# Two of a quad's four weight sums made by an accumulating DMA instead of VectorE, in the MLP of a hybrid decoder block

## The reference, cut to what matters

```python
D_MODEL, SEQ, D_FF = 2048, 256, 4 * 2048
...
u = rmsnorm(h, norm_ff_pre[l])
f = jnp.square(jax.nn.relu(u @ w_ff1[l])) @ w_ff2[l]   # (256, 8192) @ (8192, 2048), float32
h = h + rmsnorm(f, norm_ff_post[l])
```

## Time and profile before

| | us |
|---|---|
| median of three runs | 1325.41 |
| the three runs | 1325.34 to 1327.75 |
| the profiled execution, its own time | 1325.52 |
| its span, first to last instruction | 1323.7 |
| TensorE busy | 1311.4 |
| VectorE busy | 928.1 |
| ScalarE busy | 671.0 |

### The profile page before, as it was taken

One profiled execution on the slowest core, in us unless ns is written; L12 is line 12 of the kernel. 1 busy time (PEld: TensorE's weight loads), 2 busy tenths in 40 slices (PEclk: granted clock), 3 DMA queues, 4 the chain that ended last, 5 costly groups with the idle time before them and its releaser, 6 DMA issues.

```text
span 1323.7 us, 18258 instructions
## 1 busy us (share of the span) xinstructions
PE 1311.4 (99%) x6998; PEld 1116.4 (84%) x6998; DVE 928.1 (70%) x1265; ACT 671.0 (51%) x922; POOL 47.0 (4%) x92
## 2 busy tenths in 40 slices
PE   9999999999999999999999999999999999999998
PEld 8889999888888888889987888877888877888886
DVE  7766565687875555557768976579876699776554
ACT  7554453456664443454645664445454455545442
POOL 1222110000000000000000000000000000000000
PEclk9999999999999999999999999999999999999999
DMA  9766555555566666674755666646576465766653
GB/s 315 205 185 170 170 163 149 167 167 155 170 194 188 185 188 221 226 246 148 219 159 188 214 219 191 195 156 207 190 223 189 146 207 191 229 188 190 223 195 104
DMA packets 135209, 252.56 MB, mean 191 GB/s; under 512 B 8275, under 2 KB 45551, under 8 KB 134748
## 3 DMA queue, kind: packets, MB, share of 16 engines
q1 hardware_dynamic: 131216, 241.40, 58.6%
q0 software_dynamic: 2160, 4.74, 1.8%
q10 hardware_dynamic: 1756, 5.36, 1.1%
HBM read 249.29 MB, written 2.17 MB: 190 GB/s over the span
## 4 chain that ended last, share of the span: by engine, by line
PE 90%; DVE 6%; ACT 2%; DMA 1%; issue 0%; ACTq 0%; SPq 0%; DVEq 0%
PE bank L2006 16%; PE bank L1696 11%; PE bank L1698 11%; PE bank L1697 11%; PE bank L2009 8%; PE bank L1742 4%; PE bank L2056 4%; PE bank L2057 4%; PE bank L2058 4%; PE bank L1730 3%; PE bank L1731 3%; PE bank L1729 3%; PE bank L1744 2%; DVE b_lo L1536 2%; DVE s_lo L1541 1%; ACT b_hi L873 1%
## 5 line engine op out<-in xcount | busy, mean ns | idle before, releaser
L1017 DVE TENSOR_TENSOR w_lo<-raw,w_hi 128x1024 fp32r<-128x1024 f32 (+1 forms) x360 | 430.6, 1211 | 247.6 <-ACT w_hi L559 246.1
L559 ACT ACTIVATE w_hi<-raw 128x1024 fp32r<-128x1024 f32 (+1 forms) x360 | 372.4, 1048 | 292.9 <-DMA raw<-in_w_ff 173.5
L2006 PE MATMUL bank<-f_hl,w_hi 128*128 128x512 f32 x960 | 229.7, 391 | 0.0
L2006 PEld LDWEIGHTS bank<-f_hl,w_hi 128*128 128x128 f32 x960 | 176.4, 188 | 34.1
L2009 PEld LDWEIGHTS bank<-f_hl,w_lo 128*128 128x128 f32 x960 | 123.1, 191 | 4.7
L2009 PE MATMUL bank<-f_hl,w_lo 128*128 128x256 f32 x960 | 124.5, 283 | 0.0
L1696 PE MATMUL bank<-w_hi,u_hl 128*128 128x512 f32 x256 | 101.1, 395 | 0.0
L1698 PE MATMUL bank<-w_hi,u_hl 128*128 128x512 f32 x256 | 99.9, 390 | 0.0
L1697 PE MATMUL bank<-w_lo,u_hl 128*128 128x512 f32 x256 | 99.8, 390 | 0.0
L873 ACT ACTIVATE b_hi<-b_raw 128x2048 fp32r<-128x2048 f32 x24 | 46.1, 1921 | 72.7 <-DVE b_raw L1528 72.7
L1730 PE MATMUL bank<-u_hl,w_lo 128*128 128x272 f32 x288 | 82.4, 289 | 0.4 <-DVE w_lo L1017 0.4
(11 more groups left out here) (282 smaller groups left out, 2314.7 us busy)
## 6 DMA issues: line engine op xcount, KB each, us to landing
raw<-in_w_ff SPq DMA_DIRECT2D x160, 512.0 KB, 4.0
raw<-in_w_in SPq DMA_DIRECT2D x128, 512.0 KB, 3.7
s_raw<-in_w_ff SPq DMA_DIRECT2D x48, 512.0 KB, 3.9
b_raw<-in_w_ff SPq DMA_DIRECT2D x24, 1024.0 KB, 5.1
raw<-in_w_out SPq DMA_DIRECT2D x32, 512.0 KB, 4.3
raw<-in_w_branch_b SPq DMA_DIRECT2D x16, 512.0 KB, 3.8
raw<-in_w_branch_a SPq DMA_DIRECT2D x16, 512.0 KB, 3.8
xt<-in_turned_x SPq DMA_DIRECT2D x8, 272.0 KB, 5.4
```

The source lines that it names most:

```text
L559: act.activation(w_hi[:, u, :, 0:width], raw[:, u, :, 0:width], ACT.Copy).then_inc(hi_ready, 1)
L1017: dve.tensor_tensor(w_lo[:, u, :, 0:width], raw[:, u, :, 0:width], w_hi[:, u, :, 0:width].bitcast(F32), ALU.subtract).then_inc(lo_ready, 1)
L2006: ins = pe.matmul(acc[g][:], w_hi[:, u, k, cols], f_hl[:, kt, :], start=kt == 0, stop=kt == KT - 1)
```

## The change

`load_w` fetches one weight tile a second time: besides the 1 MB load, a further load of 256 KB puts the tile of slot 3 into slot 4 too. When both have landed, GpSimd issues a DMA from SBUF to SBUF that adds slots 1 and 2 onto slots 3 and 4 (512 KB, `accum_op=ALU.add`). VectorE's instruction `sum` is gone; `sums` now waits for this DMA (`b_added`). The sums have other signs than before, so four signs change at the tokens' blocks (in `activate_hidden`) and two steps of `join` subtract; the number and the sizes of these instructions are as before.

```diff
-LO_ORDER = [("sum", 0), ("sums", 0), ("first", 0), ("rest", 0), ("S", 0), ("S", 1), ("sum", 1), ("sums", 1), ("first", 1),
+LO_ORDER = [("sums", 0), ("first", 0), ("rest", 0), ("S", 0), ("S", 1), ("sums", 1), ("first", 1),
...
-    LO_ORDER += [("sum", _k), ("S", 2 * _k - 1), ("sums", _k), ("first", _k), ("rest", _k), ("S", 2 * _k)]
+    LO_ORDER += [("S", 2 * _k - 1), ("sums", _k), ("first", _k), ("rest", _k), ("S", 2 * _k)]
...
+                  .then_inc(b_landed[k % 2], 16)
+                sp.dma_start(b_raw[k % 2][:, 4, :], w_ff2[0, bass.ds(q * D + (4 * j + 1) * P, P), slice(c * 1024 + CW, c * 1024 + 1024)])\
                   .then_inc(b_landed[k % 2], 16)
...
+            for q in range(QUARTERS - 1):
+                for k in range(N_W):
+                    pool.wait_ge(b_landed[k % 2], 32 * (k // 2 + 1 + q * N_W // 2))
+                    pool.dma_start(b_raw[k % 2][:, 3:5, :], b_raw[k % 2][:, 1:3, :], accum_op=ALU.add)\
+                        .then_inc(b_added[k % 2], 16)
...
-                dve.tensor_tensor(work[:, 8, :], work[:, 3, :], work[:, 1, :], ALU.add).then_inc(hid_part, 1)
+                dve.tensor_tensor(work[:, 8, :], work[:, 3, :], work[:, 1, :], ALU.subtract).then_inc(hid_part, 1)
...
-                if kind == "sum":
-                    dve.wait_ge(b_landed[i], 16 * (n // 2 + 1) + q * (16 * N_W // 2))
-                    dve.tensor_tensor(raw_b[:, 4:2:-1, :], raw_b[:, 3:0:-2, :], raw_b[:, 2:4, :], ALU.subtract)\
-                       .then_inc(b_part, 1)
-                elif kind == "sums":
-                    dve.wait_ge(b_part, part + 1)
-                    dve.tensor_tensor(raw_b[:, 5, :], raw_b[:, 1, :], raw_b[:, 4, :], ALU.subtract).then_inc(b_part, 1)
-                    dve.wait_ge(b_part, part + 2)
-                    dve.tensor_tensor(raw_b[:, 6, :], raw_b[:, 0, :], raw_b[:, 5, :], ALU.subtract).then_inc(b_ready, 1)
+                if kind == "sums":
+                    dve.wait_ge(b_added[i], 16 * (n // 2 + 1 + q * N_W // 2))
+                    dve.tensor_tensor(raw_b[:, 5, :], raw_b[:, 1, :], raw_b[:, 4, :], ALU.add).then_inc(b_part, 1)
+                    dve.wait_ge(b_part, n + 1 + q * N_W)
+                    dve.tensor_tensor(raw_b[:, 6, :], raw_b[:, 0, :], raw_b[:, 5, :], ALU.add).then_inc(b_ready, 1)
```

More of the change, by code:

```diff
@@ L319, in hybrid_block @@
         b_landed = [sem(f"b_landed{i}") for i in range(2)]
+        b_added = [sem(f"b_added{i}") for i in range(2)]
         s_landed = [sem(f"s_landed{i}") for i in range(3)]
@@ L868, in split_item @@
                 if kind == "first":
-                    act.wait_ge(b_landed[n % 2], 16 * (n // 2 + 1) + q * (16 * N_W // 2))
+                    act.wait_ge(b_landed[n % 2], 32 * (n // 2 + 1 + q * N_W // 2))
                     act.activation(b_hi[n % 2][:, 0:3, :], b_raw[n % 2][:, 0:3, :], ACT.Copy).then_inc(hi_ready, 1)
@@ L1486, in activate_hidden @@
                 dve.wait_ge(hid_part, n + 3)
-                dve.tensor_tensor(work[:, 10, :], work[:, 0, :], work[:, 9, :], ALU.subtract).then_inc(hid_ready, 1)
+                dve.tensor_tensor(work[:, 10, :], work[:, 0, :], work[:, 9, :], ALU.add).then_inc(hid_ready, 1)
             def keep_hidden(q, j, last):
@@ L1518, in split_item @@
                 lo, hi, raw_b = b_lo[i], b_hi[i], b_raw[i]
-                part = 2 * n + q * (2 * N_W)
-                if kind == "sum":
-                    dve.wait_ge(b_landed[i], 16 * (n // 2 + 1) + q * (16 * N_W // 2))
-                    dve.tensor_tensor(raw_b[:, 4:2:-1, :], raw_b[:, 3:0:-2, :], raw_b[:, 2:4, :], ALU.subtract)\
-                       .then_inc(b_part, 1)
-                elif kind == "sums":
-                    dve.wait_ge(b_part, part + 1)
-                    dve.tensor_tensor(raw_b[:, 5, :], raw_b[:, 1, :], raw_b[:, 4, :], ALU.subtract).then_inc(b_part, 1)
-                    dve.wait_ge(b_part, part + 2)
-                    dve.tensor_tensor(raw_b[:, 6, :], raw_b[:, 0, :], raw_b[:, 5, :], ALU.subtract).then_inc(b_ready, 1)
+                if kind == "sums":
[3 more added lines that the diff above has]
+                    dve.tensor_tensor(raw_b[:, 6, :], raw_b[:, 0, :], raw_b[:, 5, :], ALU.add).then_inc(b_ready, 1)
                 elif kind == "first":
@@ L1565, in join @@
                                       for b in range(BLOCKS) for h in range(2)]
-                dst, other = ((c11, p1), (p6, p1), (p7, p6), (c21, p7), (p6, p5), (c12, p6), (p7, p5), (c22, p7))[step]
+                dst, one, other = ((c11, c11, p1), (p6, p6, p1), (p7, p7, p6), (c21, c21, p7), (p6, p5, p6), (c12, c12, p6),
+                                   (p7, p5, p7), (c22, c22, p7))[step]
                 if step:
                     dve.wait_ge(p_part, step)
-                ins = dve.tensor_tensor(dst, dst, other, ALU.add).then_inc(p_part, 1)
+                dve.tensor_tensor(dst, one, other, ALU.subtract if step in (4, 6) else ALU.add).then_inc(p_part, 1)
                 if step == 7:
```

## The result

| | before | changed |
|---|---|---|
| median | 1325.38 us | 1368.86 us |
| lowest to highest, 4 runs each | 1325.28 to 1327.75 | 1368.35 to 1371.17 |
| ratio, with its 95% interval | | 1.0327 (1.0309 to 1.0345) |
| profiled execution: time, span | 1325.52, 1323.7 | 1368.35, 1366.6 |

What follows compares the result with a forecast made beforehand. TensorE, busy 1311.4 of 1323.7 us, was taken as the bound. For L = 7, 3 x (6.3 + 2 + 5.6 - 1.0) + 2.6 = 41.3 us on 1325.52 gave 1367 us; eight in ten, 1332 to 1410.

Steps and rivals of the forecast that it cites:

- The bound: TensorE bounds the kernel; VectorE's 29 us of removed work can gain some 3 us, 10 at the very most.
- L: Accumulating DMA from semaphore to semaphore: 5.7 to 8.4 us, taken as 7; this range was the likeliest case, chance 0.45.
- the short DMA: Rival with L of 3.1 to 5.7: loop covered, only openings count, 10 us more, 1335; chance 0.20.
- its upper case: Other loads share the DMA engines; if they halve the rate, the data part is 10.6 and L 13 or so.
- Term 1, the openings: At each of three quarters' openings the chain to the sums grows by L - 0.66, 6.3 us for L = 7.
- Term 2, the clock: After a 6 us opening wait TensorE's clock falls to 1.2 GHz, slowing quad 0's remaining matmuls: 2 us per opening.
- Term 3, the loop: Two-buffer loop, quads 2 to 7: load plus L plus splitting exceeds TensorE's cover; 5.6 us of waits a quarter.
- So this blocks nothing else: VectorE's in-order queue: work behind its wait for the DMA is wanted after the sums anyway; no added cost.
- SyncE's loads at nothing: 24 more loads on SyncE's queue, 0.37 us each, cost nothing, since the next in it wait for TensorE anyway.
- The extra 256 KB: Each quad's load, with 256 KB more to fetch, lands 0.6 us later.
- Term 4, the adds: In quarters 1 and 2 `add_p` behind `rest` 4 makes TensorE wait 1.3 us, twice: 2.6 us.
- Term 5: TensorE's small waits for low parts outside the openings go away: 1.0 us a quarter comes back.

Runs made afterwards that it cites:

- the zero products: Changed kernel with matmuls against a tile of zeros filling TensorE's waits before and within quads 0 and 3: 1360.51 us, ratio 1.0284.
- the plain copy: Changed kernel with a plain SBUF-to-SBUF copy in place of the accumulating DMA, additions left out: 1346.55 us, one execution.

## Why the prediction was right, point by point

The forecast of a slower kernel, and that the openings and the two-buffer loop would make it so, held. That the time came within 2 us of the measured one is luck, as the points below show.

- **The bound.** Right. TensorE waited 2.7 us for the quads before and 29.4 after; what VectorE was spared bought nothing that shows, and putting the work back made the kernel no slower. (29 us were forecast and 25.6 came. In the records an instruction starts up to 0.1 us before the one ahead of it ends, so that 24 fewer take a little less off the sum than their own durations; that is a part of the difference.)
- **L.** Mis-sized: 7 forecast, 4.77 at the openings, 5.4 the median landing, 7.5 the longest. The term that failed is the fixed part, 3.1 us from the quickest DMA of GpSimd, which moves bytes too; the fixed part is 1.7 to 2.0. The data part, 3.95 taken within 2.6 to 5.3, is 2.8 by 5.3 us per MB, near the once-bytes end in time though both operands are read: the rate of 5.0 us per MB from the earlier trace rows was that of small DMAs, twice what a copy of this size needs. By the prediction's own cases this L belongs to the short DMA, which it had at some 1335, 34 us below what came. In the loop L isn't a fixed part plus bytes: the DMA lands some 2.5 us after the load issued before it, however long that one still takes. The prediction had the other loads only in its upper case, as halving the rate, and at nothing in the sum.
- **Term 1, the openings.** The formula held: L - 0.66 with L = 4.77 is 4.1, measured 4.23 to 4.26. The size was off with L: 12.7 us instead of 18.9.
- **Term 2, the clock.** It fell, after 3 us of waiting where the prediction had 6. At the openings 1.4 us each, against 2. What was missed is that it falls at quad 3 too, in two quarters of three. That "the time of TensorE's matmuls stay" was wrong: +16.1 us, which the zero products price at some 8.5 us of the kernel's time, give or take 5.
- **Term 3, the loop.** Total near, mechanism half wrong. The count said 5.6 us a quarter for L = 7 and none below 4.7, spread over quads 2, 3, 4, 6 and 7. Measured are 25.8 us in three quarters with the falls of the clock, and two thirds of it lie between quads 0 and 3. TensorE's waits behind the openings add up to 18.3 us, near the 16.8 of the count, but not at its places: they are at quad 3 in all quarters, at quad 7 in two, at quads 5 and 6 in one each, and none is at quads 2 and 4. The step that failed is the load: taken at 5.17 + 0.6 = 5.77 us from a free buffer on, it is 5.9 to 8.8 from issue to GpSimd's issue, and up to 3.1 late in being issued. The sum of load and L at quad 3 is 13.2 to 14.6 us, where the prediction had 12.8. So a smaller L and a slower load hid each other.
- **"So this blocks nothing else", and SyncE's loads at nothing.** Wrong. The load of quad 3 stands behind a row block's load that waits for VectorE's `hid_lo`, which stands behind a low part that waits for a load that an opening has put off. Turning two loads round gave 6.5 us, waits and clock together.
- **The extra 256 KB.** 0.52 to 0.63 us at an opening, as forecast. But the row blocks' loads became slower as well (3.9 to 4.5), and the whole is 4.5 us, not 1.8.
- **Term 4, the adds.** Not there in the changed kernel (2.6 forecast), but there, 2.24 and 1.82 us, as soon as quad 3 was no longer the latest.
- **Term 5.** 3.0 us to come back; none did. Of TensorE's small waits that had been there, quad 1's went, and larger ones elsewhere took their place.

In short: the openings were forecast at 3 x 8.3 = 24.9 us and cost 17.1; the loop with the adds, less what comes back, at 16.4 and cost 25.8. The time was right because these two errors, -7.8 and +9.4, nearly cancel: luck. Only the mechanism of the openings is confirmed as it was put.

## What to carry to other kernels

A busy engine's work is worth taking away only where the bound engine waits for it; a replacement with a longer way from load to result is paid in full wherever nothing is done meanwhile, as at a stage's opening. Transfers aren't free because their engines are half idle: with the share going from 0.55 to 0.89 the row blocks' loads landed after 4.5 us instead of 3.9, and a DMA issued behind a load was done behind it. In an in-order queue a delay reaches loads that have nothing to do with it. When a loop has two buffers, follow one buffer round from "free" to "used" with the queue's other entries in it, since that is where the slack is lost.

## What the runs showed of the hardware that was not expected

- An accumulating DMA from SBUF to SBUF of 512 KB takes 4.77 us from issue to use, a copy 2.86, half the accumulation 3.23. It occupies the 16 engines for 5.3 us per MB against 2.5. GpSimd needs 0.85 us to issue the one and 0.53 for the other.
- The same copy takes 5.2 us (median) between other loads, because from quad 2 on it lands 1.20 to 1.25 us after the load that was issued before it, in 17 of 18 cases; half the accumulation and the whole one do the same, at 1.27 and 2.5 us (medians).
- TensorE's granted clock fell to 0.50 (1.2 GHz) at each of the 24 waits of 2.2 to 3.4 us that seven of the profiles have in the second stages, from 1.1 us before the wait's end to 2.3 us after it. Shorter waits went either way. It stayed at 1.00 with a single one of 2.11 us and with pairs of 1.34 and 1.46, 1.44 and 1.51, 1.54 and 1.50 us. It fell with single ones of 1.45 and 2.00 us, and with pairs of 0.45 and 1.52 (the zero products) and 1.27 and 1.50 (the plain copy). Of the 16 us by which matmuls got longer about half showed in the time.
- VectorE and GpSimd stretch each other: 1.22 us to 3.44 and 2.29 to as much as 4.32 for VectorE, 2.38 to 4.22 for GpSimd's 128x1024.
- Open: why a needless instruction of 1.22 us per quad on VectorE makes the changed kernel 5.5 us faster. The DMAs of quad 3 are quicker there, and the next load comes later behind them.
